# A third tile of tokens by fetched rows, and one-hot rows built eight tokens at a time, in a fused encoder block

## What is computed

```python
q = (xt @ wq).reshape(T, 8, 2, 128)
s = jnp.einsum('thpe,hpke->thpk', q, keys)
sv, si = lax.top_k(s, 16)
cand = sv[:, :, 0, :, None] + sv[:, :, 1, None, :]      # 16 x 16 sums of a head
tv, ti = lax.top_k(cand, 16)                            # 16 experts of a head
eidx = take(si0 * 128 + si1, ti); g = softmax(tv)       # 8 heads x 16 = 128 experts of a token
a = einsum('cd,ced->ce', xb, utab[eidx])
out = einsum('ce,ced->cd', g * gelu(a), vtab[eidx])
```

## Time and profile before

| what | us |
|---|---|
| median of 3 runs | 4055.96 |
| lowest and highest run | 4050.32 and 4060.3 |
| the profiled execution, its own time | 4056.58 |
| its span, first to last instruction | 4054.8 |
| PE busy (share of the span) | 3708.7 (91%) |
| DVE busy | 2613.5 (64%) |
| ACT busy | 1290.4 (32%) |
| POOL busy | 1191.9 (29%) |

### The profile page before, as it was taken

One profiled execution on the slowest core, in us unless ns is written; L12 is line 12 of the kernel. 1 busy time (PEld: TensorE's weight loads), 2 busy tenths in 40 slices (PEclk: granted clock), 3 DMA queues, 4 the chain that ended last, 5 costly groups with the idle time before them and its releaser, 6 DMA issues. The chain is left out here.

```text
span 4054.8 us, 54674 instructions
## 1 busy us (share of the span) xinstructions
PE 3708.7 (91%) x19170; PEld 3237.6 (80%) x19170; DVE 2613.5 (64%) x5657; ACT 1290.4 (32%) x2513; POOL 1191.9 (29%) x797
## 2 busy tenths in 40 slices
PE   6879899998887979899999999999779999999997
PEld 3579888887666768799998988989668888888875
DVE  5563033221555421599998888889767777777777
ACT  1110122221114221223326777777622222222220
POOL 1132112211331111123334444434243333333340
PEclk9789899998999989999999999999989999999998
DMA  4751212113554222333337999999987787888882
GB/s 171 286 184 34 88 58 75 71 72 139 203 182 168 81 88 78 104 129 126 133 119 247 320 337 321 339 316 336 299 312 286 287 291 290 292 292 294 288 306 110
DMA packets 502565, 826.52 MB, mean 204 GB/s; under 512 B 289031, under 2 KB 309767, under 8 KB 496296
## 3 DMA queue, kind: packets, MB, share of 16 engines
q1 hardware_dynamic: 111704, 370.02, 25.7%
q0 software_dynamic: 84096, 318.80, 21.4%
q10 hardware_dynamic: 306576, 135.28, 13.3%
HBM read 679.30 MB, written 144.70 MB: 203 GB/s over the span
## 5 line engine op out<-in xcount | busy, mean ns | idle before, releaser
L79 PE MATMUL va_fps<-va_vt_h,va_c_h 128*128 128x512 f32 x1536 | 606.5, 395 | 62.8 <-DVE va_vt_l L2209 27.4
L80 PE MATMUL va_fps<-va_vt_l,va_c_h 128*128 128x512 f32 x1536 | 604.1, 393 | 0.0
L81 PE MATMUL va_fps<-va_vt_h,va_c_l 128*128 128x512 f32 x1536 | 603.6, 393 | 0.0
L2087 POOL DMA_INDIRECT va_rows<-in_vtab,k_pick x256 | 392.1, 1532 | 648.6 <-DVE k_big L2233 573.4
L79 PE MATMUL ga_aps<-k_u_h,k_ut_h 128*128 128x384 f32 x1152 | 403.1, 350 | 10.7 <-DVE k_ut_l L1989 7.0
L1914 ACT ACTIVATE ga_first<-ga_first,ga_gs 128x128 f16<-128x128 f16 x1152 | 357.8, 390 | 162.4 <-DVE ga_first L1973 161.9
L79 PEld LDWEIGHTS va_fps<-va_vt_h,va_c_h 128*128 128x128 f32 x1536 | 292.5, 190 | 127.7 <-issue 35.4
L81 PE MATMUL ga_aps<-k_u_h,k_ut_l 128*128 128x384 f32 x1152 | 391.1, 340 | 0.0
L80 PE MATMUL ga_aps<-k_u_l,k_ut_h 128*128 128x384 f32 x1152 | 390.4, 339 | 0.0
L2233 DVE SCALAR_TENSOR_TENSOR k_big<-va_rows,va_coef,k_big 128x1024 f32<-128x1024 f32 x254 | 321.1, 1280 | 62.8 <-DMA va_rows<-in_vtab,k_pick 60.7
L80 PEld LDWEIGHTS va_fps<-va_vt_l,va_c_h 128*128 128x128 f32 x1536 | 292.7, 191 | 60.8
(11 more groups left out here) (296 smaller groups left out, 8064.5 us busy)
## 6 DMA issues: line engine op xcount, KB each, us to landing
k_ut<-in_utab SPq DMA_DIRECT2D x129, 512.0 KB, 3.5
va_vt<-in_vtab SPq DMA_DIRECT2D x128, 512.0 KB, 6.9
va_c<-scratch_ahead SPq DMA_DIRECT2D x128, 384.0 KB, 3.4
va_wt<-scratch_gates SPq DMA_DIRECT2D x128, 384.0 KB, 5.1
hy_tab<-in_tab POOLq DMA_DIRECT2D x64, 512.0 KB, 4.8
scratch_ahead<-ga_gelu_a ACTq DMA_DIRECT2D x72, 384.0 KB, 6.5
sp_wada<-in_w_ada SPq DMA_DIRECT2D x24, 1024.0 KB, 8.4
scratch_gates<-ga_wide ACTq DMA_DIRECT2D x32, 768.0 KB, 14.6
```

The source lines that it names most:

```text
L79: nc.tensor.matmul(out, w[0], x[0], start=first, stop=False)
L80: nc.tensor.matmul(out, w[0], x[1], start=False, stop=False)
L81: return nc.tensor.matmul(out, w[1], x[0], start=False, stop=last)
L2087: nc.gpsimd.indirect_dma_start(got[:, q % SLOTS_G, :], None, vrows, picked(K, q)).then_inc(got_in[q % SLOTS_G], 16)
```

## The change

1. **One-hot rows.** The gate matrix is built for GATED = 640 tokens (5 tiles) instead of 768, in batches of 8 tokens. For a batch DVE does four two-source instructions of 128 x 1024 fp16: the first rows and the second rows by comparing, and the two weighed parts by multiplying. The indices and shares are stored twice, side by side (`at16`, `share16`, last dimension 2), so that the innermost run of every operand is a pair. ACT weighs nothing any more. The dot products stand between the comparing and the weighing of a batch; DVE works two batches ahead of PE; the buffers hold 3 batches. A block of the store is 40 tokens wide.
2. **The third tile** (tokens 256 to 383). Its products with `utab` are still made for all experts (`ahead` keeps 768 columns), but it gets no gates. DVE writes its expert numbers to `pick` and the places of its products in `ahead` to `place`. In `stage_values` its values come by fetched rows like those of the first two tiles, 384 rows in all, and its 128 products per token are fetched one fp32 number per token and instruction, 128 indirect DMAs on POOL, two behind each of the first 64 rows.
3. **Values.** PE multiplies 5 dense tiles per table tile, 3 staying and 2 passing; `c` and `wt` are 640 wide; `add_sums` runs twice a group. Rows per turn: 4 in each of turns 0 and 1, 12 in each of the next 10, 14 in each of the next 16, 16 in each of the last 2. The rows of the third tile are taken from turn 12 on, after a wait for all 128 single fetches.

```diff
@@ stage_select, ACT @@
-                    nc.scalar.activation(K["sel"][:, :, bass.ds((n - GATHERED) * P, P)],
-                                         tps[:, :].rearrange("p (a t) -> p a t", t=P), ACT.Copy).then_inc(t_ok, 1)
+                    at = bass.ds((n - VALUED) * P, P)
+                    nc.scalar.activation(K["at16"][:, :, at, :], tps[:, 0:2 * P].rearrange("p (a t) -> p a t", t=P).unsqueeze(3)
+                                         .to_broadcast([P, 2, P, 2]), ACT.Copy)
+                    nc.scalar.activation(K["sel"][:, at], tps[:, 2 * P:3 * P], ACT.Copy).then_inc(t_ok, 1)
@@ stage_gates, DVE @@
-            def one_hot(m, b):
-                dve.wait_ge(mm, m + 1)
-                for t in range(G):
...
+            def hits(m):
+                if m >= SETS:
+                    dve.wait_ge(mm, 4 + BATCH // G * (m - SETS + 1))
+                b = m % SETS
+                v.tensor_tensor(first[:, b, 0], numbers, indices(0, m), ALU.is_equal).then_inc(hot_ok, 1)
+                v.tensor_tensor(second[:, b], numbers, indices(1, m), ALU.is_equal)
+
+            def weigh(m):
+                dve.wait_ge(hot_ok, m + 1)
+                b = m % SETS
+                for part in (1, 0):
+                    last = v.tensor_tensor(first[:, b, part], first[:, b, 0], shares(part, m), ALU.mult)
+                last.then_inc(f_ok, 1)
...
-                    for b in groups_of(q):
-                        one_hot(GROUPS * i + b, b % 4)
-                        for j in rows_after(b):
-                            dot(i, j)
-                    low(1 - q % 2, TILES * i + q + 1)
+            for n in range(TILES):
+                for m in batches_of(n):
+                    if m:
+                        hits(m)
+                    for j in rows_after(m):
+                        dot(j)
+                    if m:
+                        weigh(m)
+                low(1 - n % 2, n + 1)
@@ stage_values, POOL @@
-            for q in range(GATHERED * PICKS):
+            for q in range(VALUED * PICKS):
                 pool.wait_ge(row_used, q + 1)
-                nc.gpsimd.indirect_dma_start(got[:, q % SLOTS_G, :], None, vrows, picked(K, q)).then_inc(got_in[q % SLOTS_G], 16)
+                nc.gpsimd.indirect_dma_start(got[:, q % SLOTS_G, :], None, vrows,
+                                             picked(K, *row_of(q // SLOTS_G, q % SLOTS_G))).then_inc(got_in[q % SLOTS_G], 16)
+                for p in range(2 * q, min(2 * q + 2, PICKS)):
+                    at = bass.IndirectOffsetOnAxis(ap=K["place"][:, p:p + 1], axis=0)
+                    nc.gpsimd.indirect_dma_start(single[:, p:p + 1], None, elements, at).then_inc(single_in, 16)
@@ stage_values, DVE: rows of a turn, cut at the places after t = 0 to 3 and at the end @@
-                cuts = (0, take // 2, take, 2 * take, 3 * take - 1, GT * take)
+                cuts = (0, take // 8, take // 4, take // 2, 3 * take // 4, take)
...
-            EDGE, EACH = 3, 2
+            EDGE, FEW, MANY, LAST = 4, 12, 14, 16
+            FEWS, MANYS = 5, 8
...
+            dve.wait_ge(single_in, 16 * PICKS)
+            ch.link(v.tensor_tensor(coef[:, GATHERED, :], single[:, :], K["share"][:, GATHERED, :], ALU.mult))
```

More of the change, by code:

```diff
@@ L1629, in _, with pair @@
             pe.sem_inc(a_mm, 4)
-            def pair(i, dense):
+            def pair(i):
                 for s in range(2):
@@ L1642, in pair @@
                             last.then_inc(a_mm, 1)
-                    if not dense:
+                    n = 2 * i + s
+                    if not is_dense(i, s):
                         continue
-                    n = 2 * i + s
                     hold(pe, K, sel_ok, n + 1)
@@ L1650, in pair @@
                     last.then_inc(t_mm, 1)
-            pair(0, False)
-            with pe.Fori(EARLY, PAIRS) as i:
-                pair(i, True)
+            for i in range(LOOPED):
+                pair(i)
+            with pe.Fori(LOOPED, PAIRS) as i:
+                pair(i)
         @block.scalar
         def _(act):
-            act.sem_inc(t_ok, 2 + GATHERED)
+            act.sem_inc(t_ok, 2 + VALUED)
             act.sem_inc(gelu_ok, 4)
@@ L1718, in top16, with pair @@
                 ch.link(last, K)
-            def pair(i, dense):
+            def pair(i):
                 for s in range(2):
-                    n = 2 * i + s
+                    n, dense = 2 * i + s, is_dense(i, s)
                     hold(dve, K, sc_in[s], 16 * (i + 1))
@@ new lines, in _ @@
+            for n in range(TILES):
+                s, todo = n % 2, list(groups_of(n))
+                pe.wait_ge(ut_ok, n + 3)
+                for h in range(2):
+                    pe.wait_ge(gelu_ok, 2 * n + h + 1)
+                    cut = dense_half(h)
+                    for k in range(KT):
+                        last = product3(nc, aps[:, 2 * s + h, 0:DH], (ut_h[:, s, k, :], ut_l[:, s, k, :]),
+                                        (u_h[:, k, cut], u_l[:, k, cut]), k == 0, k == KT - 1)
+                    last.then_inc(a_mm, 1)
+                    for m in (todo[:-1], todo[-1:])[h]:
+                        pe.wait_ge(f_ok, m * G // BATCH + 1)
+                        pe.wait_ge(act_out, m + 1)
+                        b = m * G // BATCH % SETS
+                        for t in range(G):
+                            for part in range(2):
+                                last = nc.tensor.matmul(ps[:, m % 4, t * NK:(t + 1) * NK], columns(second[:, b, m * G % BATCH + t, :, :]),
+                                                        columns(first[:, b, part, m * G % BATCH + t, :, :]), start=part == 0, stop=part == 1)
+                        last.then_inc(mm, 1)
@@ L1980, in dot, with of_batch, indices, shares @@
-            def dot(i, j):
-                k, turn = j % SLOTS_G, ROWS // SLOTS_G * i + j // SLOTS_G
+            shape = [P, BATCH, NK // 2, 2]
+            numbers = K["iota16"][:, :].rearrange("p (a b) -> p a b", b=2).unsqueeze(1).to_broadcast(shape)
+            def of_batch(t):
+                return t.unsqueeze(2).to_broadcast(shape)
+            def indices(part, m):
+                return of_batch(K["at16"][:, part, m * BATCH:(m + 1) * BATCH, :])
+            def shares(part, m):
+                return of_batch(share16[:, part, m * BATCH:(m + 1) * BATCH, :])
@@ L1982, in dot @@
+            scaled, pairs = K["sel"], [P, GATED, 2]
+            hits(0)
+            ch.link(v.tensor_scalar(scaled[:, :], scaled[:, :], GATE_SCALE, None, ALU.mult))
+            ch.link(v.tensor_copy(share16[:, 0], scaled[:, :].unsqueeze(2).to_broadcast(pairs)))
+            ch.link(v.tensor_tensor(share16[:, 1], scaled[:, :].unsqueeze(2).to_broadcast(pairs), share16[:, 0], ALU.subtract))
+            weigh(0)
+            def dot(j):
+                k, turn = j % SLOTS_G, j // SLOTS_G
                 dve.wait_ge(got_in[k], 16 * (turn + 1))
@@ L2031, in stage_values, with row_of @@
         vrows = T["vtab"].rearrange("i j d -> (i j) d")
-        STAY = DT // 2
-        FINAL = [STAY, 0, STAY + 1, 1, STAY + 2, 2]
-        order = [GATHERED + tt for tt in FINAL] + list(range(GATHERED))
-        last_order = list(range(GATHERED)) + [GATHERED + tt for tt in FINAL]
+        STAY, PASS = 3, 2
+        FINAL = [STAY, 0, STAY + 1, 1, 2]
+        order = [VALUED + tt for tt in FINAL] + list(range(VALUED))
+        last_order = list(range(VALUED)) + [VALUED + tt for tt in FINAL]
+        elements = S["ahead"].rearrange("n p (t a) -> (n p t) a", a=1)
+        ALTERNATE = PICKS // SLOTS_G
+        def row_of(turn, k):
+            if isinstance(turn, int) and turn < ALTERNATE:
+                return k % 2, 2 * turn + k // 2
+            return (0, 2, 1, 2)[k], (2 * (turn - ALTERNATE) + k // 2 if k % 2 else turn + PICKS // 2 - ALTERNATE)
         def banks(tt):
```

245 lines of the change are left out of this document (111 added, 134 removed).

## The result

| | before | after |
|---|---|---|
| median of 4 runs each, us | 4055.09 | 4234.32 |
| lowest and highest run | 4050.32 and 4060.3 | 4228.71 and 4238.75 |
| profiled execution, its span | 4056.58, 4054.8 | 4236.37, 4234.6 |

The ratio is 1.0441, 95% interval 1.0422 to 1.046: the change makes the kernel 4.4% slower. The forecast was 4074, its range ended at 4145. The sign was right, the size was not.

The account below looks back on a forecast made before the run. PE was taken to bound the values stage, and PE, DVE and ACT together the gates stage. From 4056.6 us, -66 for the gates stage and +83 for the values stage gave 4074 us, range 3975 to 4145.

Parts of the forecast that it names:

- The price T of a one-hot instruction: Gates stage, DVE: each of 320 two-source fp16 instructions of 1024 elements taken at 0.65 us, between bounds 0.67 and 1.14.
- rival on T: Gates stage, two slower rivals: fp32 rate, 1.14 us, 4154 us, chance 0.12; repeated pairs read slowly, near 0.95, 4125 us, 0.06.
- The gates stage: Gates stage: 704 us instead of 770, so -66 us, with ACT's 44.5 us of waits gone.
- 678 + 18 + 8 for clock and small waits: Gates stage sum: PE's work 678 us, idle at the start 18, clock and small waits 8, together 704.
- the 330 GB/s: Gates stage before the change: the DMA engines' rate; 344 GB/s would be needed after, under 367 of a full window.
- Turns 0 and 1: Values stage, first two turns: 55 us instead of 81.1, so -26.
- The single fetches: Values stage, 4.67 turns: POOL takes 4.65 us per row and its two fetches; 250 us instead of 152, +98.
- The full turns: Values stage: sixteen turns of 14 rows at 34 us, +22; 5.33 turns of 12 rows at 30.5 us, -11.
- Slots: four rows in flight: Values stage: 7.0 us to landing, 0.3 issue, 1.2 use per row; 14 rows in 30 us at best.
- The first: Faster rival, values stage: single fetches hold POOL under 0.5 us each, so don't pace it; 3966 us, chance 0.16.
- The second: Faster rival, values stage: full turns at their limit, 30 us for 14 rows, 27.5 for 12; 3987 us, chance 0.15.

Follow-up runs that it names:

- without rows: The changed kernel without the 256 fetched rows and dot products of the gates stage, dot products set to zero: 4152.5 us, the stage 684.
- both causes mended: The changed kernel with gates stored as runs of 5 KB per partition and the low part ahead of the dot products: 4177.1 us, the stage 709.

## Why the prediction was right or wrong

**The price T of a one-hot instruction: right.** In the changed kernel they follow one another at 2500.05 - 2499.44 = 0.61 and 2500.65 - 2500.05 = 0.60 us, where I took 0.65:

```profile
2499.44 0.69 DVE L1983 TENSOR_TENSOR ga_first<-k_iota,k_at 128x1024 f16<-128x1024 f16 x1 [0.19 <-PE ga_ps L1902]
2500.05 0.68 DVE L1984 TENSOR_TENSOR ga_second<-k_iota,k_at 128x1024 f16<-128x1024 f16 x1
2500.65 1.22 DVE L2004 SCALAR_TENSOR_TENSOR ga_rows<-ga_rows,k_u_row 128x1024 f32<-128x1024 f32 x1
```

The rule that the prediction cites from the Trainium skill (VectorE: DVE Perf Modes, The perf-mode tier table), 0.60, holds, and neither rival on T did: repeated pairs cost nothing.

**The gates stage: -66 forecast, -12 measured.** PE's work was right (684 us without rows, 709 with both causes mended). The step that failed is "678 + 18 + 8 for clock and small waits": with ACT's weighing gone I counted its 44.5 us as won, and only 8 us for clock and small waits in their place. The runs show 64.2 us of PE waiting for the low part. The start, which I had put at 18, is one of these waits, 16.3 us; the other 48 had only the 8. They come from the dot products in front of the low part, for whose rows DVE waits 99 us. Two things lie behind that. I took the 330 GB/s for a load with room up to 367, since I read the transfers in bytes; in packets there was no room, and the DMA share in that very row was 1.10 before and is 1.08 after. But the DMA engines were as busy before, when DVE waited only 19 us for rows (2140 to 2900 us), so the packets alone do not explain the rise. New with the change is that the dot products stand three or four together between the instructions of a batch, with four slots for their rows; spreading them halved the waits for rows. More slots in this stage were not tried, so how much of the rise is the slots' stays open.

**Turns 0 and 1: right**, 49.5 us for 55.

**The single fetches: right**, +90 for +98. POOL's timeline shows what I had assumed, a fetch of 128 numbers at the price of a row:

```profile
3100.71 0.95 POOL L2118 DMA_INDIRECT va_rows<-in_vtab,k_pick  x1 [0.30 <-issue]
3101.96 0.95 POOL L2122 DMA_INDIRECT va_single<-scratch_ahead,k_place  x1 [0.30 <-issue]
3103.22 1.16 POOL L2122 DMA_INDIRECT va_single<-scratch_ahead,k_place  x1 [0.30 <-issue]
3104.69 1.56 POOL L2118 DMA_INDIRECT va_rows<-in_vtab,k_pick  x1 [0.30 <-issue]
```

But their removal gives 75 us, not 90: beneath them the slots would have held the turns at some 36 us, not at PE's 32.6. That the sum came so near is in part luck: a row and its two fetches took about 4.4 us instead of 4.65, and the 15 us of the slots, which the sum did not have there, made up for it.

**The full turns: +22 and -11 forecast, +108 and +20 measured.** The step that failed is "Slots: four rows in flight, each 7.0 us to landing plus 0.3 of issue and 1.2 of use, 14 rows in 30 us at best". A slot's round took 39.3 x 4 / 14 = 11.2 us instead of 8.5. Two things were left out. POOL issues the fetches of freed slots one behind another, at 1.54 us in the mean and 0.30 between them, where I had counted 0.3 us for one, and a landed row waits in DVE's own order behind the 12.7 us of other work in a turn. "At best" was meant as a bound and then used as if it were nearly reached; turn 28, with 12 rows in 35.4 us, was already held by its slots (with 7 of them it took 32.6), at 2.95 us a row, and 14 rows at that are 41 us. The measured 39.3 are nearer to that than to my 34. I had gone by DVE's work instead, 29.3 us in turn 28 and 29.5 in a turn of 14 rows, and even so put 14 rows below the 35.4 us that 12 had taken.

**The rivals.** All four fell. The first had a single fetch below 0.5 us, and its instruction takes 0.95 and 1.16 above. Both on T fell with the 0.60. The second, full turns at their limit of 30 us, is what 7 slots give (31), not 4.

## What to carry to other kernels

A ring of k buffers gives a row no faster than its whole round divided by k, and the round holds the issue of the fetches before it and the consumer's other work, not only the landing. The round is no constant either: it was longer with 5 slots than with 4. Read it from the tightest turn that the trace has, in us per row, and before work is moved onto such a ring, ask for more buffers: here three, borrowed from a later phase, were worth 184 us. Count a store's packets as well as its bytes: here a store that shrank by a sixth through shorter runs left its queue at 48.8% of the engines' time, from 50.5%.

## What the runs showed that I had not expected

- One core moved 388 GB/s for 400 us with 7 slots (above), not only in single windows of 10 us. The 358 GB/s that the prediction cites from the Trainium skill (DMA: Bandwidth & Descriptors, Specifications) are no limit in this run, in which one core works.
- Some of POOL's issues of a row are stretched beside DVE's work. In one turn of 14 rows of the changed kernel:

```profile
3828.22 4.35 POOL L2118 DMA_INDIRECT va_rows<-in_vtab,k_pick  x1 [2.51 <-DVE k_big L2269]
3832.88 0.95 POOL L2118 DMA_INDIRECT va_rows<-in_vtab,k_pick  x1 [0.30 <-issue]
3834.14 0.95 POOL L2118 DMA_INDIRECT va_rows<-in_vtab,k_pick  x1 [0.30 <-issue]
3835.39 0.94 POOL L2118 DMA_INDIRECT va_rows<-in_vtab,k_pick  x1 [0.30 <-issue]
```

DVE worked from 3818.57 to 3834.1 without a gap and idled to 3838.25. The first issue, beside five of its instructions, took 4.35 us; the two in its idle time took 0.95 and 0.94, but so did the one at 3832.88, beside one long instruction. The Trainium skill (SBUF — State Buffer, SBUF: two separate sides) tells of a port that DVE and POOL share and that an instruction of DVE with two inputs in SBUF can keep from POOL while POOL's own instruction reads SBUF; the 4.35 us fit it and the 0.95 beside DVE does not speak for it; no run here changed DVE's instructions alone, so the cause is not shown. With 7 slots the issues into the old four slots were as long, 1601 ns in the mean (about 1280 into the three new ones), and DVE waited 0.9 us for rows in 400.
- Half the bytes of a row nearly halved its flight, but only where the issue was short. In the chain from 3440 to 4000 us, the run with half rows has 29 landings, counted from the start of the issue: 16 of 3.5 to 4.6 us, whose issues took 0.95 us, and 13 of 8.0 to 9.0 us, whose issues took 2.76 or 4.36 us. The whole rows of the changed kernel took 5.7 to 8.3 us there, 6.9 in the mean, all but one behind issues of 0.94 to 1.44 us. That fits stretched issues as a part of why halving the bytes gave only 2.6 us a turn; no run took them away by themselves.
